# Hybrid decoder layer: second block of the first right-hand quarter loaded by itself, one operand sum on GpSimd, first products in another order

## The reference

```
hn = rms_norm(x, norm1_g)
z  = gelu(hn @ w_in)                     # 1024x1024 @ 1024x4096
u, v = split(z)                          # 2048 columns each
v  = layer_norm(v) * ln_g
sv = tril(w_s) @ v per chunk of 128 rows and group of 256 columns, + b_s
x  = x + (u * sv) @ w_out                # 2048 -> 1024
x  = x + square(relu(rms_norm(x, norm2_g) @ w1)) @ w2
out = rms_norm(x, final_g)
```

## Time and profile before

| | us |
|---|---|
| median of 3 runs | 1124.45 (1124.19 to 1124.59) |
| the profiled execution's own time | 1126.03 |
| its span, first to last instruction | 1124.2 |
| PE busy | 1114.8 (99%) |
| DVE busy | 785.9 (70%) |
| ACT busy | 569.4 (51%) |
| POOL busy | 23.5 (2%) |
| DMA moved | 193.80 MB, 172 GB/s on average |

### The profile page before, as it was taken

One profiled execution on the slowest core, in us unless ns is written; L12 is line 12 of the kernel. 1 busy time (PEld: TensorE's weight loads), 2 busy tenths in 40 slices (PEclk: granted clock), 3 DMA queues, 4 the chain that ended last, 5 costly groups with the idle time before them and its releaser, 6 DMA issues.

```text
span 1124.2 us, 13090 instructions
## 1 busy us (share of the span) xinstructions
PE 1114.8 (99%) x5088; PEld 928.2 (83%) x5088; DVE 785.9 (70%) x833; ACT 569.4 (51%) x870; POOL 23.5 (2%) x17
## 2 busy tenths in 40 slices
PE   8999999999999999999999999999999999999997
PEld 7888888888888888888888888888888888888886
DVE  4976655688779986678658547455599575677666
ACT  6774444553554334565774365454653433433456
POOL 0000000000000000000000000000000000000240
PEclk9999999999999999999999999999999999999999
DMA  8173253272865494731353635527878354343213
GB/s 294 45 210 127 94 187 113 75 244 93 316 250 221 159 358 144 217 113 38 113 187 126 211 113 183 193 108 272 293 292 305 111 226 187 113 150 113 78 73 150
DMA packets 81933, 193.80 MB, mean 172 GB/s; under 512 B 4528, under 2 KB 10704, under 8 KB 75216
## 3 DMA queue, kind: packets, MB, share of 16 engines
q1 hardware_dynamic: 81392, 192.69, 48.7%
q10 hardware_dynamic: 480, 0.28, 0.1%
HBM read 134.24 MB, written 58.72 MB: 172 GB/s over the span
## 4 chain that ended last, share of the span: by engine, by line
PE 98%; DMA 1%; ACT 0%; DVE 0%; ACTq 0%; issue 0%
PE banks L427 32%; PE banks L432 32%; PE banks L431 32%; PE banks L496 3%; PE banks L541 1%; DMA gain_rows<-in_a_ln_g_dram 1%; DVE rows L1516 0%; ACT spare L1133 0%; PE banks L503 0%; PE banks L552 0%; PE banks L523 0%; ACT rows L1325 0%; ACT o_rms L1333 0%; ACTq L922 0%; ACTq L924 0%
## 5 line engine op out<-in xcount | busy, mean ns | idle before, releaser
L984 ACT ACTIVATE pair_high<-left_and_right 128x1024 fp32r<-128x1024 f32 x168 | 177.2, 1060 | 244.4 <-PE banks L427 193.4
L1378 DVE TENSOR_TENSOR ring_low<-left_and_right,ring_high 128x512 fp32r<-128x512 f32 x224 | 152.6, 692 | 192.7 <-ACT ring_high L954 192.3
L1386 DVE TENSOR_TENSOR pair_low<-left_and_right,pair_high 128x1024 fp32r<-128x1024 f32 x168 | 204.1, 1230 | 113.9 <-ACT pair_high L984 113.9
L954 ACT ACTIVATE ring_high<-left_and_right 128x512 fp32r<-128x512 f32 x224 | 138.4, 629 | 251.2 <-PE banks L427 155.9
L427 PE MATMUL banks<-pair_high 128*128 128x512 f32 x672 | 261.9, 390 | 0.0
L432 PE MATMUL banks<-pair_high,pair_low 128*128 128x512 f32 x672 | 261.5, 389 | 0.0
L431 PE MATMUL banks<-pair_low,pair_high 128*128 128x512 f32 x672 | 261.4, 389 | 0.0
L427 PE MATMUL banks<-s_high,ring_high 128*128 128x512 f32 x384 | 149.6, 389 | 0.0
L431 PE MATMUL banks<-s_low,ring_high 128*128 128x512 f32 x384 | 149.4, 389 | 0.0
L432 PE MATMUL banks<-s_high,ring_low 128*128 128x512 f32 x384 | 149.4, 389 | 0.0
L427 PEld LDWEIGHTS banks<-pair_high 128*128 128x128 f32 x672 | 126.1, 188 | 26.6 <-DVE pair_low L1386 0.3
(11 more groups left out here) (116 smaller groups left out, 1223.5 us busy)
## 6 DMA issues: line engine op xcount, KB each, us to landing
left_and_right<-sums SPq DMA_DIRECT2D x40, 1024.0 KB, 7.1
left_and_right<-in_mlp_w_dram SPq DMA_DIRECT2D x36, 1024.0 KB, 6.5
sums<-rows SPq DMA_DIRECT2D x34, 1024.0 KB, 5.4
left_and_right<-in_a_w_in_dram SPq DMA_DIRECT2D x19, 1024.0 KB, 6.2
v_blocks<-rows SPq DMA_DIRECT2D x8, 1024.0 KB, 4.5
left_and_right<-in_a_w_out_dram SPq DMA_DIRECT2D x8, 1024.0 KB, 9.7
rows<-in_x_dram SPq DMA_DIRECT2D x7, 1024.0 KB, 8.7
spare<-v_blocks SPq DMA_DIRECT2D x6, 1024.0 KB, 6.9
```

The costliest lines, as they stand in the source:

```text
L954: nc.scalar.activation(ring_high[k][:, :], right_place(n, pos)[:, k, :], ACT.Copy)\
L984: nc.scalar.activation(pair_high[pair_entry(d, pos, k)][:, :, :], pair_of(d, pos, k), ACT.Copy)\
L1378: nc.vector.tensor_tensor(ring_low[k][:, :], right_place(n, pos)[:, k, :], ring_high[k][:, :].bitcast(F32), ALU.subtract).then_inc(low_don ...
L1386: nc.vector.tensor_tensor(pair_low[e][:, :, :], pair_of(d, pos, k), pair_high[e][:, :, :].bitcast(F32), ALU.subtract).then_inc(low_done, 1)
```

## The change

- The load of blocks 1 to 3 of b11 is cut into block 1 (with a semaphore of its own, `second_landed`) and blocks 2 and 3. ACT's `split_high` of unit 1 waits for block 1 alone.
- b12 is loaded behind b21 instead of behind a12.
- norm2's gain in its second layout (`g2_fours`) is loaded by SP behind the bias, not by ACT between two other small loads.
- PE has 4 fillers, the transpose of norm1's gain, 2 fillers, `first_turn(0)` and `(1)`. `turn_gains` stands behind unit 0. The 3 later fillers are gone.
- Unit 0 is computed by `first_unit`: 4 products high x high for the 4 banks as soon as the two high parts are there, then 4 with the left low part, then 4 with the right low part.
- DVE copies the gains out of bank 7 behind `first_low(1)`, and does `sum_t(0,0)` behind the sum s2.
- `sum_t(0,2)` leaves DVE. GpSimd computes it, ahead of the mask of `ws_nat`, once b22 has landed and `sum_t(0,0)` is done; ACT's `split_high(0,4,k)` waits for it (`t3_pooled`).

```diff
 def t_sum(n, i):
-    return 4 * n + i + 1 + (8 if n >= 4 else 0)
+    return 4 * n + i + 1 + (8 if n >= 4 else 0) - (1 if (n, i) > (0, 2) else 0)
...
+            def first_unit():
+                banks = set_of(slot(0, 0))
+                rows_high, rows_low = high["a11"][:, 0, :], low["a11"][:, 0, :]
+                pe.wait_ge(combo_high, 1)
+                pe.wait_ge(high_done, unit(0, 0, 0) + 1)
+                for m in range(4):
+                    begin_fill(("product", 0, 0), banks[m])
+                    c = slice(m * P, (m + 1) * P)
+                    mm = nc.tensor.matmul(ps[:, banks[m], :], rows_high[:, c], ring_high[0][:, :], start=True,
+                                          stop=False, skip_group_check=True)
+                    if m == 0:
+                        mm.then_inc(unit_begun, 1)
+                pe.wait_ge(combo_low, 1)
...                                          # 4 products rows_low x ring_high[0]
+                pe.wait_ge(low_done, unit(0, 0, 0) + 1)
...                                          # 4 products rows_high x ring_low[0]
@@ single(n) on PE
-                        single_unit(n, pos, k)
                         if n == 0 and pos == 0 and k == 0:
+                            first_unit()
+                        else:
+                            single_unit(n, pos, k)
+                        if n == 0 and pos == 0 and k == 0:
+                            turn_gains()
                             first_turn(2)
                             first_turn(3)
@@ ahead of single(0) on PE
-            warm(2 * WARM_UP)
+            warm(4)
             turn_g1()
+            warm(2)
             first_turn(0)
             first_turn(1)
-            turn_gains()
-            warm(3)
@@ SP
-            load(("b11", 0), quarter[0][:, 1:4, :], weight(0, "b11")[:, 1:4, :], quarter_landed[0], "quarter0")
+            sp.dma_start(quarter[0][:, 1:2, :], weight(0, "b11")[:, 1:2, :]).then_inc(second_landed, 16)
+            load(("b11", 0), quarter[0][:, 2:4, :], weight(0, "b11")[:, 2:4, :], quarter_landed[0], "quarter0")
             load_x("a12", 0, NB, NB)
-            load_weight(0, "b12")
             load_x("a21", 4, 0, NB)
             load_x("a22", 4, NB, NB)
             load_weight(0, "b21")
+            load_weight(0, "b12")
             sp.wait_ge(*landed["b21", 0])
             load_weight(0, "b22")
...                                          # ws_nat, bias
+            sp.dma_start(g2_fours[:, :, :], norm2_g.rearrange("a (h p j) -> p (a h) j", h=2, j=4)).then_inc(g2_landed, 16)
@@ ACT: its issue of g2_fours between the two loads of gain_rows is gone; in right_ready
+                elif (n, pos) == (0, 4):
+                    act.wait_ge(t3_pooled, 1)
@@ ACT, split_high
                 if u == 0:
                     act.wait_ge(first_landed, 16)
+                elif u == 1:
+                    act.wait_ge(second_landed, 16)
@@ DVE, single(0)
-                    sum_t(0, 0)
                     low_combo(0, "a12")
                     for k in range(4):
                         s3_rows(k)
                     split_low(0, 1, 0)
                     split_low(0, 1, 1)
                     sum_combo(0, "s2")
+                    sum_t(0, 0)
                     split_low(0, 1, 2)
                     split_low(0, 1, 3)
...
                     low_combo(0, "s3")
-                    sum_t(0, 2)
                     split_low(0, 3, 2)
@@ DVE, ahead of single(0)
             split_low(0, 0, 0)
+            first_low(1)
             filled(dve, "gains", 7)
             nc.vector.tensor_copy(gains[:, KT:], ps[:, 7, 0:KT + JT]).then_inc(drained[7], 1)
-            first_low(1)
             split_low(0, 0, 1)
@@ POOL, ahead of the mask of ws_nat
+            q = {b: quarter[i][:, :, :] for b, i in places(0).items()}
+            pool.wait_ge(*landed["b22", 0])
+            pool.wait_ge(t_summed, t_sum(0, 0))
+            nc.gpsimd.tensor_tensor(q["b12"], q["b22"], q["b12"], ALU.subtract).then_inc(t3_pooled, 1)
```

More of the change, by code:

```diff
@@ L22 @@
 QT = NB // P
-WARM_UP = 4
 EPS = 1e-6
@@ L72, in t_sum @@
 def t_sum(n, i):
-    return 4 * n + i + 1 + (8 if n >= 4 else 0)
+    return 4 * n + i + 1 + (8 if n >= 4 else 0) - (1 if (n, i) > (0, 2) else 0)
 def t_sum_double(d, i):
-    return (16 if d == 0 else 40 + 8 * (d - 1)) + i + 1
+    return (15 if d == 0 else 39 + 8 * (d - 1)) + i + 1
 def acted_count(n, blk, m):
@@ L308, in trunk @@
         t_summed = sem("t_summed")
+        t3_pooled = sem("t3_pooled")
         relued = sem("relued")
@@ L322, in trunk @@
         first_landed = sem("first_landed")
+        second_landed = sem("second_landed")
         x_summed = sem("x_summed")
@@ L458, in single_unit @@
                                  start, stop, m == 0)
+            def first_unit():
[11 more added lines that the diff above has]
+                pe.wait_ge(combo_low, 1)
+                for m in range(4):
+                    c = slice(m * P, (m + 1) * P)
+                    nc.tensor.matmul(ps[:, banks[m], :], rows_low[:, c], ring_high[0][:, :], start=False,
+                                     stop=False, skip_group_check=True)
+                pe.wait_ge(low_done, unit(0, 0, 0) + 1)
+                for m in range(4):
+                    c = slice(m * P, (m + 1) * P)
+                    nc.tensor.matmul(ps[:, banks[m], :], rows_high[:, c], ring_low[0][:, :], start=False,
+                                     stop=False, skip_group_check=True)
             def double_unit(d, pos, k):
@@ L923, in _ @@
             act.dma_start(gain_rows[0:KT, :], norm2_g.rearrange("a (k p) -> (a k) p", p=P)).then_inc(gains_landed, 16)
-            act.dma_start(g2_fours[:, :, :], norm2_g.rearrange("a (h p j) -> p (a h) j", h=2, j=4)).then_inc(g2_landed, 16)
             act.dma_start(gain_rows[KT:, :], a_ln_g.rearrange("a (k p) -> (a k) p", p=P)).then_inc(gains_landed, 16)
```

## The result

The changed kernel takes 1131.75 us (median of 4 runs, 1129.23 to 1132.55), the kernel before, run beside it, 1124.35 us (1124.19 to 1124.59): ratio 1.0061, 95% interval 1.0045 to 1.0077. It is 7.4 us **slower**, outside the range of the prediction (1122.4 to 1128.9). The profiled execution took 1132.55 us with a span of 1130.7, 6.5 more than before. The four spans of the changed kernel are 1127.4, 1129.4, 1130.6 and 1130.7 us, so the profiled execution is its longest; why they differ is taken up at after_again.

A forecast was written before the change was run, and what follows sets the result against it. PE, with DVE setting the pace as much between 30 and 50 us. DVE's low part for (0,3,0): 48.69 - 3.2 + 2.2 - 0.9 + 4.35 + 0.9 = 52.05 against 50.6, so 1124.45 + 1.5 = 1126.0 us; range 1122.4 to 1128.9.

The forecast's parts named there:

- I take it that a first sum is late by about 6 us again: GpSimd's sum, released near 31.1 us, would stop DVE only around 37 us, behind the low part of (0,2,0).
- the 41 that the prediction named as a sign of being wrong: The prediction called itself wrong if unit (0,2,0) began before 36.5 us or after 41 us.
- GpSimd at once: Rival: POOL's sum gets the port at DVE's next boundary, all ahead of (0,2,0); 1127.6 us, 1129.2 with half clock; chance 0.22.
- the earlier start: First product 2.3 us earlier and s2 up to 3.5 us earlier on DVE; taken as 3.2 us.
- The price of the sum: `sum_t(0,2)` on POOL makes DVE lose 0 to 4.6 us once; taken as 4.35 us.
- The exclusive hold: POOL and DVE sums exclude each other from a shared port for a whole instruction; read from a 2.00 against 1.2 us row.
- The lower end of my own range: The start is worth only 2.3 us if the half clock lasts over 6 of unit 0's products, losing 1.2 us.
- +2.2 for `sum_t(0,0)`: Moved behind s2 into DVE's busy stretch, the sum adds 2.2 us ahead of `split_low(0,1,2)`, without cover.
- The -0.9 for the mask: POOL's mask no longer stretches `split_low(0,1,2)` on DVE, saving 0.9 us; taken back behind the late POOL sum.
- Harmless: Rival: POOL's sum waits until DVE reads PSUM and falls into slack; 1122.4 us, chance 0.20.
- The clock falls: Rival: POOL's sum comes late and the 3 us PE stall brings back the half clock, +1.0 us: 1127.0 us; chance 0.13.

The follow-up runs named there:

- after_again: The changed kernel run and profiled once more with no edit: 1129.22 us, ratio 1.0046, profiled span 1127.4 us.
- e2: The kernel before with one edit, `sum_t(0,2)` on GpSimd ahead of the mask: 1128.95 us, ratio 1.0038.
- e8: The changed kernel with `sum_t(0,2)` back on DVE and 13 added GpSimd products of 128x512 on an unused buffer: 1127.86 us in one execution.
- e10: As e8 without the last added product, and with one more directly ahead of the real product near 1061 us: 1126.02 us in one execution.
- e1: The changed kernel with `sum_t(0,2)` back on DVE at its old place: 1125.26 us, ratio 1.0007, profiled span 1123.2 us.
- e6: The changed kernel with GpSimd's sum cut into four pieces of 128x512: 1131.08 us, ratio 1.0056.
- e5: The changed kernel with GpSimd's sum held back to the low part of unit (0,2,3), the mask going first: 1125.70 us, ratio 1.0014.
- e7: e1 with GpSimd's mask of `ws_nat` held back to the low part of unit (0,3,3): 1124.13 us, ratio 0.9994.

## Why the prediction was wrong

**The step that failed** is the one printed bold in the part on `sum_t(0,2)`: "I take it that a first sum is late by about 6 us again". The sum was late by 0.45 us in the changed kernel and by 1.0 in e2, both times up to the next boundary of DVE's instructions, so its hold fell ahead of (0,2,0), where DVE has 0.16 us in hand, and not behind it. (0,2,0) began at 44.46 and 42.73, past the 41 that the prediction named as a sign of being wrong. The mechanism was the rival "GpSimd at once", which had a chance of 0.22 and 1127.6 to 1129.2 us. The evidence was there: of two rows that bore on it, the mask's (same place, a 2.00 us record with the port taken at the next boundary) was nearer to the case than the product at 1060 us, which shows a lateness that e8 and e10 find in that stretch and at none of the three other places where an added product met DVE.

**A second term failed as well**: the earlier start, put at 3.2 us and worth about 1.4 in the usual execution (below).

**The price of the sum** was right: 4.35 foreseen, 4.43 from the port's granting to its end, 4.39 on DVE's rows, 4.2 between e1's and after_again's spans. The exclusive hold was right too.

**The start.** First product 7.33 (7.2 foreseen), and s2 at 26.64 to 26.67 wherever the full clock was recorded by 7 us with the new loads (e1, after_again, e6, e10): the 3.2 us against 29.87. Where it came at 11.2 to 11.6 us (the profiled changed kernel, e5, e7, e8) s2 stood at 28.39 to 28.64: 1.7 to 2.0 us less. The lower end of my own range, which had this mechanism, was 2.3. A second thing is larger for the median. The 3.2 us are counted from a profiled execution of before that lost time to the half clock at 9.5 to 12.9 us (1.6 us by the prediction's own count of 8 products), and the median of its other spans is 1.6 us below the profiled one. e7 has the moved sum and no collision (+2.2 - 0.9 = +1.3), and its usual span is 1122.2 to 1122.3 against before's 1122.4 in that session: on that basis the start is worth about 1.4 us, an estimate. The constant distance from (0,2,0) to the end says the same: a span of 1122.4 puts before's (0,2,0) at 37.8 and, by the profiled distance of 9.8, its s2 near 28.1, which is 1.4 us behind 26.65. Adding the constant 1.8 between span and time did not see this. What the shorter executions of before look like at their start is not shown, as neither profile caught one. So the 1.4 us are what is left over, not a row that anybody read.

**The moved sum and the mask.** +2.2 for `sum_t(0,0)` stands in every trace that has it behind s2 (30.59 to 32.87). The -0.9 for the mask is given back: in the changed kernel the mask moved behind GpSimd's sum and cost 0.68 there, still ahead of (0,2,0); without that sum it still met a low part (2.18 for two, e1). The prediction had the 0.9 come back behind the late sum, and so only on the path to (0,3,0). e7 shows its price: 1.1 us by the medians, 1.0 by the usual spans (1123.2 and 1122.2).

**The sum, put right**, in spans, from the usual 1122.4 of before: start -1.4, moved sum +2.2, mask 0 net, GpSimd +4.2: 1127.4, the commonest span of the changed kernel. That is +5.0 where the forecast had +1.5. Of the 3.5 between them 1.7 are the step above (the rival "at once" came to +3.2) and 1.8 the start, so even that rival, right in its mechanism, is 1.8 us short: its 1127.6 stands against 1129.2 for the usual execution. A late clock at the start and half clock behind the stall add 1.7 each in some executions: 1130.8, against 1130.7 in the profiled one. The median of the first session lies near this end, that of the second at the other.

**The other rivals.** "Harmless" needed DVE at PSUM work while POOL reads; e5 made that so, and the sum's own cost fell to some 0.7 us. "The clock falls" was right as a mechanism, +1.7 us at 45.3 to 48.7 us in the profiled run, where the rival had 1.0 and "at once" 1.6 at most.

## What to carry to other kernels

Before work is moved from VectorE to GpSimd, look at what VectorE does at the moment when GpSimd's instruction is released: if it is a run of instructions with two SBUF inputs on the path, the move costs GpSimd's whole 4.4 us instead of saving 2.3, and cutting it up does not help; release it where VectorE reads PSUM. When two rows disagree on when an engine gets in, take the one from the same stretch. When the profiled execution is a microsecond or two off the median run, look for what in it may be particular to that execution (here the clock in the first 13 us) before a saving is counted from its rows.

## What the runs showed of the hardware

- Under contention GpSimd and VectorE alternate instruction by instruction: four GpSimd sums of 128x512, of some 1.15 us each on the port, took 9.88 us together (e6). At 1058 to 1067 us that does not hold: there GpSimd was refused at four boundaries in a row (7.57 in the changed kernel, 7.63 in e10, with other operands and a GpSimd just used). The Trainium skill (SBUF — State Buffer, section "Who interferes with whom") says issue order decides who blocks; the rows at 33, 31 and 605 us agree, those at 1060 do not.
- One and the same start, with its first product at 7.32 to 7.40 us in ten profiled executions, has its full clock recorded at 5.7 to 7.0 us in some executions and at 11.2 to 11.6 in others, and nothing between; what decides it these runs don't tell. In the second kind the clock column reads 1.00 from 7 to 11 us all the same, while products stand 0.43 to 0.46 us apart: the spacing of products is the better witness there.
- The same half clock of 3.4 us is free if the unit under it is ahead of the engine that it will wait for (after_again), and costs 1.7 us if it falls behind the stall (the changed kernel).
